# The opening of a two-block fp32 transformer kernel: x requested between modulation tiles, the modulation summed in two steps, the first weight remainder on GpSimd

## What is computed

```python
mod = (c @ w_mod[l] + b_mod[l]).reshape(B, N_MOD, D)
shift_m, scale_m, gate_m = mod[:, 0, None], mod[:, 1, None], mod[:, 2, None]
...
h = rms_norm(x, g_pre_mix[l]) * (1 + scale_m) + shift_m
proj = h @ w_in[l]
```

## Time and profile before

| | us |
|---|---|
| median of 3 runs | 2405.12 |
| lowest, highest | 2404.49, 2405.45 |
| the profiled execution | 2404.69 |
| its span, first to last instruction | 2403.0 |
| mean granted clock of TensorE | 0.999 of full speed |

### The profile page before, as it was taken

One profiled execution on the slowest core, in us unless ns is written; L12 is line 12 of the kernel. 1 busy time (PEld: TensorE's weight loads), 2 busy tenths in 40 slices (PEclk: granted clock), 3 DMA queues, 4 the chain that ended last, 5 costly groups with the idle time before them and its releaser, 6 DMA issues.

```text
span 2403.0 us, 31168 instructions
## 1 busy us (share of the span) xinstructions
PE 2373.3 (99%) x11010; PEld 1972.4 (82%) x11010; DVE 1598.3 (67%) x1950; ACT 1127.0 (47%) x1421; POOL 9.8 (0%) x18
## 2 busy tenths in 40 slices
PE   6999999999999999999999999999999999999998
PEld 5888788888888888888888888888888888888887
DVE  7998899899787665445444464545655557777664
ACT  4544545544464444444444454445544444444554
POOL 0001000000000000000000000000000000000000
PEclk9999999999999999999999999999999999999999
DMA  9985469999857875555555555665555554444454
GB/s 392 378 313 200 156 259 354 329 341 355 296 193 265 285 254 182 195 184 192 184 193 194 193 188 189 202 203 189 192 192 191 185 189 159 145 168 156 159 191 158
DMA packets 148138, 537.20 MB, mean 224 GB/s; under 512 B 16704, under 2 KB 17984, under 8 KB 147648
## 3 DMA queue, kind: packets, MB, share of 16 engines
q1 hardware_dynamic: 145584, 528.28, 63.7%
q10 hardware_dynamic: 2448, 7.47, 0.9%
HBM read 533.59 MB, written 2.10 MB: 223 GB/s over the span
## 4 chain that ended last, share of the span: by engine, by line
PE 97%; DVE 2%; DMA 1%; ACT 0%; issue 0%; SPq 0%; ACTq 0%; DVEq 0%
PE acc L1850 29%; PE acc L1852 29%; PE acc L1851 29%; PE tb L1932 2%; PE tb L2343 1%; DVE macc L1263 1%; PE tb L1850 1%; PE tb L1852 1%; PE tb L1851 1%; PE acc L1902 0%; PE acc L1901 0%; PE acc L1900 0%; PE tb L2346 0%; PE tb L2066 0%; DMA start_raw<-in_wa_dram 0%
## 5 line engine op out<-in xcount | busy, mean ns | idle before, releaser
L1091 DVE TENSOR_TENSOR lo<-raw,hi 128x1024 fp32r<-128x1024 f32 (+1 forms) x812 | 971.9, 1208 | 603.1 <-ACT hi L532 600.5
L532 ACT ACTIVATE hi<-raw 128x1024 fp32r<-128x1024 f32 (+1 forms) x812 | 845.6, 1049 | 892.7 <-PE acc L1852 722.3
L1850 PE MATMUL acc<-hi,Hh 128*128 128x512 f32 x1968 | 778.6, 396 | 2.0 <-DVE Hl L1582 0.7
L1852 PE MATMUL acc<-hi,Hl 128*128 128x512 f32 x1968 | 767.4, 390 | 0.0
L1851 PE MATMUL acc<-lo,Hh 128*128 128x512 f32 x1968 | 766.3, 389 | 0.0
L1850 PEld LDWEIGHTS acc<-hi,Hh 128*128 128x128 f32 x1968 | 369.7, 188 | 80.1 <-issue 5.5
L1852 PEld LDWEIGHTS acc<-hi,Hl 128*128 128x128 f32 x1968 | 369.4, 188 | 78.0
L1851 PEld LDWEIGHTS acc<-lo,Hh 128*128 128x128 f32 x1968 | 369.8, 188 | 75.7 <-issue 1.4
L1850 PE MATMUL acc<-hi,hbh 128*128 128x512 f32 x512 | 204.8, 400 | 0.0
L1852 PE MATMUL acc<-hi,hbl 128*128 128x512 f32 x512 | 200.2, 391 | 0.0
L1851 PE MATMUL acc<-lo,hbh 128*128 128x512 f32 x512 | 199.7, 390 | 0.0
(11 more groups left out here) (310 smaller groups left out, 1934.7 us busy)
## 6 DMA issues: line engine op xcount, KB each, us to landing
raw<-in_wa_dram SPq DMA_DIRECT2D x680, 512.0 KB, 4.3
late_raw<-in_wa_dram SPq DMA_DIRECT2D x96, 512.0 KB, 5.5
raw<-in_wb_dram SPq DMA_DIRECT2D x96, 512.0 KB, 4.2
start_raw<-in_wa_dram SPq DMA_DIRECT2D x64, 512.0 KB, 6.9
raw<-in_wc_dram SPq DMA_DIRECT2D x64, 512.0 KB, 3.4
x<-in_x_dram SPq DMA_DIRECT2D x2, 1024.0 KB, 6.3
x<-in_x_dram ACTq DMA_DIRECT2D x1, 2048.0 KB, 9.3
nf<-in_row_dram ACTq DMA_DIRECT2D x2, 512.0 KB, 4.4
```

The source lines that it names most:

```text
L532: act.activation(hi[:, s, 0:n], raw[:, r, 0:n], ACT.Copy).then_inc(hi_ready, 1)
L1091: dve.tensor_tensor(lo[:, s, 0:n], raw[:, r, 0:n], hi[:, s, 0:n].bitcast(F32), ALU.subtract)\
L1850: pe.matmul(dst(tt), a, hi[:, s, w], start=first and i == 0, stop=False)
L1852: mm = pe.matmul(dst(tt), b, hi[:, s, w], start=False, stop=last and i == kts - 1)
```

## The change

SyncE requests the first half of x behind modulation tile 1 and the second behind tile 3; VectorE's norm comes behind tile 3. The eight products of the first quarter's sum run in the order 0, 1, 4, 5, then 2, 3, 6, 7: the first four (scale and shift of slices 0 and 1) go to bank 3 of `tb` and are reported by themselves, the others go to bank 3 of `acc`. VectorE makes bias and gain for two slices at a time, ScalarE the slices of `Hh` two at a time, with unit 1's `hi` between them. The `lo` of unit 0 is made by GpSimd. All counts of `mod_read` and `mod_taken` rise by one (`SUMS`). The fillers of TensorE are as before.

```diff
--- before.py
+++ after.py
@@ -71,6 +71,7 @@
 C_UNITS = 64
 QUARTERS = 4
 START_UNITS = QUARTERS * KD
+SUMS = QUARTERS + 1
 
 
 PHASE = 19
@@ -456,9 +457,10 @@
                 for i in range(first + turns * RING, units):
                     load(w[i])
 
-            for tt in range(TT):
-                sp.dma_start(x[:, tt, :], x_in[:, tt, :]).then_inc(x_tile[tt], 16)
             for m in range(KD):
+                if m in (2, 4):
+                    tt = m // 2 - 1
+                    sp.dma_start(x[:, tt, :], x_in[:, tt, :]).then_inc(x_tile[tt], 16)
                 load_start(m)
             for unit in range(FFN0):
                 for q, kt in START_AT.get(unit, ()):
@@ -481,6 +483,9 @@
         @block.gpsimd
         def _(pool):
             pool.memset(ones[:], 1.0).then_inc(memory_set, 1)
+
+            pool.wait_ge(hi_ready, 1)
+            pool.tensor_tensor(lo[:, 0, :], raw[:, 0, :], hi[:, 0, :].bitcast(F32), ALU.subtract).then_inc(unit_split, 1)
 
             pool.wait_ge(row_loaded, 4 * 16)
             pool.memset(kT2[:], 0.0).then_inc(memory_set, 1)
@@ -624,19 +629,25 @@
                     b = 2 * (part % 2) + tt
                     act.activation(part_at(part, tt), acc[:, b, :], ACT.Copy).then_inc(acc_free[b], 1)
 
+            def scaled_in(k, dst):
+                shift = 8 * (k // 4) + 4 + k % 4
+                return act.activation(dst[:, k, :], xnT[:, k, :], ACT.Identity, scale=fA[:, k:k + 1], bias=modfm[:, shift:shift + 1])
+
+            def scale_pair(i):
+
+                act.wait_ge(fa_ready, i + 1)
+                for k in (2 * i, 2 * i + 1):
+                    ins = scaled_in(k, Hh)
+                ins.then_inc(in_hi, 1)
+
             def scale_in(q):
 
-                act.wait_ge(fa_ready, q + 1)
+                act.wait_ge(fa_ready, q + 2)
                 for k in range(4 * q, 4 * q + 4):
-                    shift = 8 * q + 4 + k % 4
-                    ins = act.activation(Hh[:, k, :] if q == 0 else xnT[:, k, :], xnT[:, k, :], ACT.Identity,
-                                         scale=fA[:, k:k + 1], bias=modfm[:, shift:shift + 1])
-                    if q == 0 and k % 2 == 1:
-                        ins.then_inc(in_hi, 1)
-                if q > 0:
-                    ins.then_inc(in_scaled, 1)
-                    act.wait_ge(in_scaled, q)
-                    act.activation(Hh[:, 4 * q:4 * q + 4, :], xnT[:, 4 * q:4 * q + 4, :], ACT.Copy).then_inc(in_hi, 1)
+                    ins = scaled_in(k, xnT)
+                ins.then_inc(in_scaled, 1)
+                act.wait_ge(in_scaled, q)
+                act.activation(Hh[:, 4 * q:4 * q + 4, :], xnT[:, 4 * q:4 * q + 4, :], ACT.Copy).then_inc(in_hi, 1)
 
             act.dma_start(ident[:], table_in[:, 0:P]).then_inc(ident_loaded, 16)
             act.wait_ge(memory_set, 1)
@@ -656,8 +667,10 @@
             for b in range(3):
 
                 act.wait_ge(tb_free[b], 1 + len(range(b, KD // 2, 3)))
-            split_to(START_LEAD)
-            scale_in(0)
+            split_to(1)
+            scale_pair(0)
+            split_to(2)
+            scale_pair(1)
             at = P
             for dst, n in ((ropeC, TT * HD), (ropeS, TT * HD), (iropeC, TT * IROPE), (iropeS, TT * IROPE)):
                 act.dma_start(dst[:], table_in[:, at:at + n].rearrange("p (a b) -> p a b", a=TT)).then_inc(const_in, 16)
@@ -1106,7 +1119,7 @@
 
                     summed = 2 * (block - 1 if block < LATE_WIDE - 2 else LATE_WIDE - 2)
                     if summed > 0:
-                        dve.wait_ge(mod_read, QUARTERS + 2 + summed)
+                        dve.wait_ge(mod_read, SUMS + 2 + summed)
                 else:
 
                     if block < LATE_WIDE - 2:
@@ -1133,14 +1146,14 @@
 
             def add_up_block():
 
-                dve.wait_ge(mod_read, c.at("took") + (QUARTERS + 2 + 1))
+                dve.wait_ge(mod_read, c.at("took") + (SUMS + 2 + 1))
                 dve.tensor_reduce(modfm[:, cols(c.at("took") * 4 + START_BLOCKS * 4, 4)],
                                   tb[:, 3, :].rearrange("p (q s) -> p q s", q=4), AX_X, ALU.add).then_inc(mod_taken, 1)
                 c.up("took")
 
             def add_bias(start, n):
 
-                dve.wait_ge(mod_taken, c.at("took") + QUARTERS)
+                dve.wait_ge(mod_taken, c.at("took") + SUMS)
                 chain(dve.tensor_tensor(modfm[:, start:start + n], modfm[:, start:start + n], vec("b_mod", start, n), ALU.add))
 
             def gated_gain(gate, gain):
@@ -1251,7 +1264,8 @@
 
                 dst = macc[:, q % 2, :]
                 if kt == 0:
-                    dve.wait_ge(mod_read, q + 1)
+                    if q > 1:
+                        dve.wait_ge(mod_read, q + 2)
                 else:
                     dve.wait_ge(mod_used, q * KD + kt)
                 m = q * KD + kt
@@ -1268,12 +1282,23 @@
             def start_input(q):
 
 
-                dve.wait_ge(mod_read, 2 + q + 1)
+                dve.wait_ge(mod_read, 2 + q + 2)
                 m, k = q * 8, q * 4
                 dve.tensor_tensor(modfm[:, m:m + 8], tb[:, 3, m:m + 8], vec("b_mod", m, 8), ALU.add).then_inc(mod_taken, 1)
-                dve.wait_ge(mod_taken, q + 1)
+                dve.wait_ge(mod_taken, q + 2)
                 dve.scalar_tensor_tensor(fA[:, k:k + 4], modfm[:, m:m + 4], 1.0, vec("g_pre_mix", k, 4),
                                          ALU.add, ALU.mult).then_inc(fa_ready, 1)
+
+            def start_pair_input(i):
+
+                k = 2 * i
+                pair = lambda ap: ap.rearrange("p (s k) -> p s k", s=2)[:, :, k:k + 2]
+                dve.wait_ge(mod_read, 2 + i + 1)
+                dve.tensor_tensor(pair(modfm[:, 0:8]), pair((tb, acc)[i][:, 3, 0:8]), pair(vec("b_mod", 0, 8)), ALU.add).then_inc(mod_taken, 1)
+                dve.wait_ge(mod_taken, i + 1)
+                dve.scalar_tensor_tensor(fA[:, k:k + 2], modfm[:, k:k + 2], 1.0, vec("g_pre_mix", k, 2),
+                                         ALU.add, ALU.mult).then_inc(fa_ready, 1)
+                dve.wait_ge(fa_ready, i + 1)
 
             def start_pair(i):
 
@@ -1294,16 +1319,18 @@
             dve.wait_ge(fm_loaded, 16)
             for kt in range(KD):
                 start_unit(0, kt)
-                if kt == 1:
+                if kt == 3:
                     dve.wait_ge(ssq_ready, c.up("ssq"))
                     rms(D)
             for b in range(3):
 
                 dve.wait_ge(tb_free[b], 1 + len(range(b, KD // 2, 3)))
-            split_to(1)
-            start_input(0)
-            dve.wait_ge(fa_ready, 1)
+            start_pair_input(0)
             start_pair(0)
+            start_pair_input(1)
+            c.up("unit")
+            c.up("raw")
+            dve.wait_ge(unit_split, 1)
             split_to(2)
             start_pair(1)
             def add_part(q, part, pair, last):
@@ -1954,7 +1981,7 @@
                     pe.wait_ge(mod_used, START_UNITS + (block // 2 + 1) * KD)
                 if block >= LATE_BLOCKS - 4:
                     taken(3)
-                pe.wait_ge(mod_taken, c.at("late") + QUARTERS)
+                pe.wait_ge(mod_taken, c.at("late") + SUMS)
                 for q in range(4):
                     at = (block % 2 * 4 + q) * P
                     ins = pe.transpose(tb[:, 3, q * P:(q + 1) * P], late_sums(block // 2)[:, at:at + P], ident[:])
@@ -1977,9 +2004,12 @@
             def start_sum(q):
 
                 pe.wait_ge(mod_used, (q + 1) * KD)
-                for j in range(8):
-                    ins = pe.matmul(tb[:, 3, cols(q * 8 + j, 1)], macc[:, q % 2, j * P:(j + 1) * P], ones[:],
+                for j in (0, 1, 4, 5, 2, 3, 6, 7) if q == 0 else range(8):
+                    bank = acc if q == 0 and j % 4 > 1 else tb
+                    ins = pe.matmul(bank[:, 3, cols(q * 8 + j, 1)], macc[:, q % 2, j * P:(j + 1) * P], ones[:],
                                     start=True, stop=True)
+                    if q == 0 and j == 5:
+                        ins.then_inc(mod_read, 1)
                 ins.then_inc(mod_read, 1)
 
             pe.wait_ge(xn_ready, TT)
```

## The result

The changed kernel took 2408.61 us in the median of 21 runs (2406.84 to 2409.19), the kernel before 2404.88 (2404.36 to 2405.62): 3.7 us more, a ratio of 1.0015 with a 95% interval of 1.0009 to 1.0021. That is inside the range of 2404.9 to 2409.0 and under the 0.2% that were called the same. It is 1.2 us more than the rise of 2.5 that was forecast, and 1.0 us above the forecast time of 2407.6, at the very edge of the 2406.8 to 2408.6 that was given for the forecast case by itself. The profiled execution has a span of 2406.9 us where it was 2403.0.

A forecast was written before the change was run, and what follows sets the result against it. TensorE was taken to bound the kernel from the first weight unit on, so opening delays reach the end undiminished. +2.95 - 0.85 + 0.40 = +2.50 us on 2405.12 gave 2407.6, range 2404.9 to 2409.0.

The forecast's parts named there:

- the fillers take over: TensorE's opening: the 63 filler transposes, started later by x, end at 34.96 and hold the sum instead of VectorE.
- Rival (a): Opening: fillers don't hold the sum, VectorE's last modulation tile at 32.67 does; +0.26 us, 2405.4; 9%.
- When x arrives: DMA in the opening: x's second half lands at 14.15 instead of 9.04, at 1.28 us per 512 KB.
- the forecast's 2.95: Start of the sum on TensorE: held by the fillers, at 34.96 instead of 32.01, +2.95 us.
- No hole in DMA: DMA in the opening: enough transfers stay in flight while VectorE waits; weight units land as before, the first at 30.96.
- The two-step sum: Sum over partitions: VectorE reads after 8 of 16 passes, 0.85 us sooner; the second pair of slices costs 0.40.
- net of -0.45: From the sum's start to the third weight unit: -0.85 us for the earlier read, +0.40 for the second pair.
- the exclusion: VectorE and GpSimd: a VectorE instruction with two inputs in SBUF and a reading GpSimd instruction exclude each other.
- rival (b): Inside Rival (a): VectorE's last tile holds GpSimd back, which holds VectorE's gain until 35.1; 1.1 us later, 2406.5; 4%.
- GpSimd's remainder: Unit 0's remainder on GpSimd: from 32.1 to 34.5, 2.4 us long, with 3.9 us of cover.
- Rival (d): GpSimd's remainder of unit 0 is slow, at the upper bound of 12.4 us: +8.3 us, 2413.4; 4%.
- Rival (c): Opening: VectorE isn't held at the norm and only DMA binds, tile 15 summed at 30.8; -1.6 us, 2403.6; 4%.

The follow-up runs named there:

- e1: The changed kernel with 45 fillers ahead of the sum instead of 63 (WARM_ROW 11 instead of 9): 2407.11 us.
- e11: The changed kernel with 54 fillers ahead of the sum instead of 63 (WARM_ROW 10): 2407.57 us.
- e7: The kernel before with 81 fillers instead of 63 (WARM_ROW 7): 2405.46 us.
- e8: The kernel before with both halves of x requested behind modulation tile 1, the norm still behind tile 1: 2407.05 us.
- e12: The kernel before with requests in the order x's first half, tile 0, second half, tile 1, the norm still behind tile 1: 2404.83 us.
- e6: The kernel before with both halves of x requested behind modulation tile 0 instead of ahead of it: 2406.38 us.
- e5: The changed kernel with x requested first again and the norm behind tile 1, keeping two-step sum and GpSimd: 2405.07 us.
- e2: The kernel before with only x's requests moved between the tiles and the norm behind tile 3: 2408.62 us.
- e9: The changed kernel with 45 fillers and unit 0's remainder back on VectorE: 2407.86 us.
- e3: The kernel before with only the two-step sum, VectorE making unit 0's remainder: 2404.51 us.
- e4: The kernel before with only unit 0's remainder moved to GpSimd: 2404.81 us.
- e10: The kernel before with the two-step sum, the norm's reciprocal behind tile 2 and 54 fillers: 2404.55 us.

## Why the prediction was right, and by how much it was off

**That the fillers take over: right.** e1, e11 and e7 move the time by moving their number alone (-1.5, -1.0 and +0.6 us), and in the changed kernel's trace the sum follows the last filler without a wait, 1.8 us behind the last tile. Rival (a), VectorE as the holder, is what comes next when they are out of the way (e1, e8).

**When x arrives: the term that was too small.** The step "x's second half at 9.04 + 4 x 1.28 = 14.15" came out at 15.72, 1.57 later. Order and bytes were right, the rate wasn't: 1.28 us for 512 KB was read where DMA runs full, and was used from the first transfer on. Tile 0 came at 4.90 (5.3 forecast), tile 1 at 8.04 (6.6). In the kernel before, and in e12, x stood first and the stretch of 4 to 6 us ran at full rate, so no row of before could show this. e6 has only this in it: tile 1 1.68 us late, and 1.5 us in the median.

**What follows.** The norm released VectorE at 18.39 (16.85), the fillers began at 29.14 (28.03; the transposes were 0.43 us quicker this time), ended at 36.00 after 6.86 us (6.93 forecast), and the sum stood at 35.97 (34.96). So the forecast's 2.95 was 3.96, and this 1.01 us is nearly all of the difference between the 2.50 forecast and the 3.57 found at the third unit. That the quicker transposes hid 0.43 us of the late x is luck: with the transposes of the kernel before, the rise would have been 4.0.

**"No hole in DMA": only partly right.** The rate from 22 to 31 us was 311 to 389 GB/s instead of about 410, and unit 0 was converted at 33.71 instead of 30.96, where the forecast had "as before". That fewer tiles were asked for ahead while VectorE stood in the norm may be the reason, but isn't shown to be: in e11, with the same order of requests and the same wait of VectorE, the rate was 365 to 414 GB/s and unit 0 was converted at 32.11. It cost nothing here, as the first product came at 39.50, but it moved GpSimd's subtraction.

**The two-step sum: right in its distances, wrong in company.** From the sum's start the first sums were read after 1.19 us (1.13 forecast), the first product came 2.34 later as forecast, and the third unit 5.84 behind the second remainder (5.83). Its net of -0.45 is there as 0.39 (9.62 us from the sum to the third unit instead of 10.01), and only because GpSimd was done at 37.20, before the gain at 37.36. That is luck: the forecast had GpSimd from 32.1 to 34.5 and 1.6 us to spare, and 0.16 were left. In the kernel with x first (e5) the exclusion takes the gain away, which rival (b) had priced at 1.1 us and which measured 0.9, and 1.5 in e1.

**GpSimd's remainder: right in its length, not in its place.** It started at 34.85 instead of 32.1, since unit 0 came late. It took 2.35 us, against 2.4 in the forecast, between bounds of 1.1 and 12.4; its first two-input instruction is not dear, so the 1.546 us row stands for that other instruction alone. The Trainium skill (GPSIMD Engine Reference, Engine selection) has about twice VectorE's time; 2.35 over 1.22 is 1.9, so the trace agrees. Rival (d) fell with it. Rival (c) fell with x's landing.

## To carry to other kernels

A filler that keeps an engine busy is work on that engine: it stands in program order, and when what starts it comes later, it delays what is behind it by all that no longer fits into the wait that it used to fill, unless it is shortened with it. Here 6.86 us of fillers held the sum 1.8 us behind the last tile. When requests are reordered, count when the consumer that everything else hangs on is served, not when the first one is; bytes ahead of the last transfer stay the same. And before work is moved to GpSimd, look at what VectorE is to do meanwhile with two inputs in memory.

## Not expected of the hardware

A 512 KB modulation tile as the first large transfer was followed, between 4 and 6 us, by rates of 102 to 328 GB/s, in all seven kernels that began so (the changed one, e1, e2, e6, e8, e9, e11); with a half of x first (1024 KB), in the other seven, the rates were 356 to 451. TensorE's first transposes of x took 0.86 us for four, for two to five groups, and then came faster, at a granted clock of 1.00 throughout. That is 0.21 us each, the pace that the fillers had in e1 at a granted clock of 0.50 (3.45 us for 16). And waits of 0.3 us or so between rows of fillers or ahead of the sum were followed, in the profiles of e1, e3, e6, e9 and e12, by a granted clock of 0.50, the 1.2 GHz level, for 2 to 3 us; the profiles of the kernel before, e4, e5, e8 and e10 had such waits and no fall. Where the fillers ran up to the sum without a wait (the changed kernel, e2, e7, e11) it stayed at 1.00. What the fall cost, by the distance from the gain to the third unit, was 0.8 us in e3, 1.0 in e9, 0.7 in e6, 0.5 in e12, and nothing in e1, where VectorE was held longer anyway. So leaving out fillers gained 1.0 and 1.5 us in the medians, and opened a wait behind which the clock may fall. That the wait is what lets it fall, and why it fell behind some of them only, isn't shown.
